# Hybrid encoder layer with a top-2 mixture of experts: the first expert's weight units in buffers of their own, the loop's next units loaded early, and its down product from raw units

## The reference, cut to what matters

```python
h = rmsnorm(x, norm_ffn[i])
# hier_moe: the best of 4 groups, then the best 2 of its 4 experts; 16 experts in all
for e in range(N_EXPERTS):
    gu = t @ w_gate_up[e]                                   # 1024 -> 2 * 256
    y = (jax.nn.silu(gu[:, :D_EXPERT]) * gu[:, D_EXPERT:]) @ w_down[e]   # 256 -> 1024
    out = out + combine[:, e:e + 1] * y
x = x + hier_moe(...)
x = x + jax.nn.sigmoid(x @ w_ple_gate[i]) * rmsnorm(p[i] @ w_ple_proj[i], ple_norm[i])
```

## Time and profile before

| | us |
|---|---|
| median of 3 runs | 652.64 (651.5 to 652.98) |
| the profiled execution, its own time | 650.8 |
| its span, first to last instruction | 649.0 |
| PE busy | 617.4 (95%) |
| DVE busy | 413.1 (64%) |
| ACT busy | 337.6 (52%) |
| POOL busy | 63.1 (10%) |
| mean granted clock of PE | 0.986 of full |

### The profile page before, as it was taken

How to read it: one execution, slowest core, us unless ns; L and a number is a source line. 1 busy time by engine, 2 the same in 40 slices (tenths; PEclk the granted TensorE clock), 3 DMA queues, 4 the chain that set the end, 5 groups by cost and what they waited for, 6 DMA issues and landing times.

```text
span 649.0 us, 8478 instructions
## 1 busy us (share of the span) xinstructions
PE 617.4 (95%) x3088; PEld 501.4 (77%) x3088; DVE 413.1 (64%) x758; ACT 337.6 (52%) x609; POOL 63.1 (10%) x76
## 2 busy tenths in 40 slices
PE   5999999999999999999999986799999999879997
PEld 4878888888887777888788865687777787668885
DVE  6322265444533665656786977788988987866672
ACT  7751222321323665655555664588888886941111
POOL 0000000000000000110011132212122121110000
PEclk9999999999999999999999997799999999989999
DMA  9913205030312430100112659899999999533511
GB/s 346 369 51 149 97 2 191 32 98 1 97 33 65 171 131 0 66 33 34 66 66 81 224 177 342 292 403 400 394 402 397 401 365 339 159 146 114 167 44 66
DMA packets 34506, 113.74 MB, mean 175 GB/s; under 512 B 5240, under 2 KB 5880, under 8 KB 34464
## 3 DMA queue, kind: packets, MB, share of 16 engines
q1 hardware_dynamic: 28752, 99.99, 42.1%
q0 software_dynamic: 4752, 12.59, 5.1%
q10 hardware_dynamic: 960, 0.60, 0.4%
HBM read 103.17 MB, written 14.71 MB: 182 GB/s over the span
## 4 chain that ended last, share of the span: by engine, by line
PE 73%; DVE 13%; ACT 6%; DMA 4%; issue 3%; SPq 0%; ACTq 0%; DVEq 0%; POOLq 0%
PE bank L468 21%; PE bank L470 19%; PE bank L469 19%; DVE w_split L447 7%; PE bank L1721 5%; ACT w_split L441 3%; PE bank L1748 3%; PE bank L1767 3%; DVE moe_xT L1571 2%; PE bank L1729 2%; PE bank L1876 1%; DMA w_raw<-in_w_moe 1%; DMA pick<-moe_rows 1%; ACT s L840 1%; DMA moe_x<-h_rows,slot_token 1%
## 5 line engine op out<-in xcount | busy, mean ns | idle before, releaser
L468 PE MATMUL bank<-w_split,h_T_prompt 128*128 128x512 f32 x192 | 77.6, 404 | 6.7 <-DVE w_split L1186 6.7
L470 PE MATMUL bank<-w_split,h_T_prompt 128*128 128x512 f32 x192 | 75.9, 395 | 0.0
L469 PE MATMUL bank<-w_split,h_T_prompt 128*128 128x512 f32 x192 | 75.8, 395 | 0.0
L463 DVE TENSOR_TENSOR w_split<-w_raw,w_split 128x1024 fp32r<-128x1024 f32 x33 | 40.2, 1221 | 42.2 <-ACT w_split L458 42.1
L447 DVE TENSOR_TENSOR w_split<-w_raw,w_split 128x1024 fp32r<-128x1024 f32 x48 | 56.6, 1220 | 4.8 <-ACT w_split L441 4.7
L468 PE MATMUL bank<-w_split,moe_xT 128*128 128x512 f32 x120 | 50.9, 424 | 6.0 <-DVE moe_xT L1571 3.8
L447 DVE TENSOR_TENSOR w_split<-w_raw_more,w_split 128x1024 fp32r<-128x1024 f32 x44 | 51.8, 1219 | 3.6 <-ACT w_split L441 3.6
L441 ACT ACTIVATE w_split<-w_raw 128x1024 fp32r<-128x1024 f32 x48 | 48.8, 1061 | 0.4
L468 PEld LDWEIGHTS bank<-w_split,h_T_prompt 128*128 128x128 f32 x192 | 36.6, 191 | 15.0 <-DVE w_split L1186 6.7
L470 PE MATMUL bank<-w_split,moe_xT 128*128 128x512 f32 x120 | 48.1, 401 | 0.0
L469 PE MATMUL bank<-w_split,moe_xT 128*128 128x512 f32 x120 | 47.9, 400 | 0.0
(11 more groups left out here) (270 smaller groups left out, 1362.1 us busy)
## 6 DMA issues: line engine op xcount, KB each, us to landing
w_raw<-in_w_moe SPq DMA_DIRECT2D x54, 512.0 KB, 7.4
w_raw_more<-in_w_moe SPq DMA_DIRECT2D x42, 512.0 KB, 8.6
w_raw<-in_w_in SPq DMA_DIRECT2D x24, 512.0 KB, 6.1
pick<-moe_rows SPq DMA_DIRECT2D x10, 512.0 KB, 4.5
w_raw<-in_w_out SPq DMA_DIRECT2D x8, 512.0 KB, 3.4
toep<-bias_table SPq DMA_DIRECT2D x4, 896.0 KB, 7.5
x_row<-in_x SPq DMA_DIRECT2D x6, 512.0 KB, 10.0
x_again<-in_x SPq DMA_DIRECT2D x6, 512.0 KB, 3.2
```

Of the source, the lines that this page charges most:

```text
L463: nc.vector.tensor_tensor(W[:, u % WS, 1], raw(u)[0], f(W[:, u % WS, 0]), ALU.subtract).then_inc(lo_done, 1)
L468: nc.tensor.matmul(out, hi, whi, start=first, stop=False)
L469: nc.tensor.matmul(out, lo, whi, start=False, stop=False)
L470: return nc.tensor.matmul(out, hi, wlo, start=False, stop=last)
```

## The change

The units of expert 15 get raw buffers of their own (`first_raw`, units 0 to 3, in region A), loaded during the attention stage; units 4 and 5 stay in `RAW` and are not split at all. With `RAW` units 0 to 3 free, SP loads the next set as soon as the trip count is known. The down product of a loop trip is made in float32 from the raw units and an unsplit `act32`, so ACT and DVE don't split units 4 and 5 of a trip, nor the transposed product; these raw buffers are refilled once the down half that reads them is done. After the last trip, two more entries of the table name expert 2, so the loop loads units 0 to 3 of t = 3. GpSimd starts the gather of the next loop tile ahead of the loop and at the end of each trip. The order of ACT, DVE and SP follows.

```diff
-C_N = C_SEQ + OVER_TILES + 1
+SETS = OVER_TILES + 2
+C_N = C_SEQ + SETS
-            sb("x2_T_last", [P, KD, P], F32, "A", 8192)]
+            sb("x2_T_last", [P, KD, P], F32, "RAW", 20480)]
-        h2_last = sb("h2_last", [P, D], F32, "A")
+        h2_last = sb("h2_last", [P, D], F32, "RAW", 4096)
+        first_raw = [sb(f"w_raw_first{j}", [P, 2, N], F32, "A", o_)
+                     for j, o_ in enumerate((0, 4096, 40960, 8192))]
+        act32 = sb("loop_actT", [P, 2, P], F32, "X")
-        FIRST_HI = (4, 5, 1, 0, 2, 3)
+        FIRST_HI = (0, 1, 3, 2)
 # SP, ahead of the loop
+            def first_unit(j):
+                sp.dma_start(first_raw[j][:], w_moe[E - 1, j]).then_inc(raw(MOE0 + j)[1], 16)
             for i in range(1, TILES):
+                if i == TILES - 1:
+                    sp.wait_ge(d_s, 2 * (NI - 1))
+                    for j in (0, 1, 3):
+                        first_unit(j)
                 x_again(i)
...
+                sp.wait_ge(lo_done, MOE0 + j - RS + 1)
+                sp.dma_start(RAW[:, (MOE0 + j) % RS], w_moe[E - 1, j]).then_inc(lp_ld[j], 16)
             store_h2(TILES - 2)
+            sp.wait_ge(pe_wo, 2 * TILES - 1)
+            first_unit(2)
             store_h2(TILES - 1)
+            sp.wait_ge(pe_wo, 2 * TILES)
+            moe_unit((2, 1))
+            sp.wait_ge(d_h2, 2 * TILES)
+            moe_unit((2, 3))
             sp.wait_ge(lp_xg, 16)
-            for j in range(2):
+            sp.wait_ge(d_route, 1)
+            n = sp.value_load(trips[0:1, 0:1], min_val=1, max_val=OVER_TILES + 1)
+            src = expert(0)
+            for j in range(4):
+                set_unit(src, j)
+            for j in (2, 0):
+                sp.wait_ge(lp_lo, {0: 4, 2: 3}[j])
                 moe_unit((2, j))
             with sp.Fori(0, n) as i:
-                for j in range(6):
-                    sp.wait_ge(lp_lo, i * 6 + (j + 1))
-                    sp.dma_start(RAW[:, (MOE0 + j) % RS], src[j]).then_inc(lp_ld[j], 16)
-            for j in range(2, 4):
-                moe_unit((2, j))
-            for j in range(4):
-                sp.wait_ge(lp_lo, n * 6 + (j + 1))
+                src = expert(i)
+                for j in range(4, 6):
+                    sp.wait_ge(lp_y, i * 2 + (j - 3))
+                    set_unit(src, j)
+                src = expert(i + 1)
+                for j in range(4):
+                    sp.wait_ge(lp_lo, i * 4 + (j + 5))
+                    set_unit(src, j)
+            for j in range(4, 6):
+                sp.wait_ge(lp_lo, n * 4 + (j + 1))
                 moe_unit((3, j))
             sp.wait_ge(pe_gu, 1)
             for j in range(4, 6):
                 moe_unit((2, j))
 # POOL, ahead of the loop (in the trip the same gather stands after the put)
+            pool.sem_inc(lp_free, 1)
+            pool.tensor_copy(now_u[:], src_u[:, bass.ds(column(0), 1)]).then_inc(g_now, 1)
+            pool.wait_ge(g_now, 2)
+            pool.wait_ge(lp_xt, 2)
+            pool.sem_inc(g_go, 1)
+            fetch(xg[0], now_u[:], lp_xg)
             for i in range(2):
                 pool.wait_ge(gch, 3 + i)
                 gather_x(2 + i)
 # ACT
             ple_out(5)
+            act.wait_ge(lp_lo, 1)
             xT_hi(1)
...
-                out_actT_hi().then_inc(lp_aat, 1)
+                act.activation(act32[:], bank[3][:, 0:DE].rearrange("p (k t) -> p k t", k=2),
+                               ACT.Copy).then_inc(lp_aat, 1)
...
-                for j in range(4, 6):
-                    loop_hi(i, j)
+            for j in range(4, 6):
+                loop_hi(n, j)
             moe_hi((2, 0))
             moe_hi((2, 1))
 # DVE: the table (12 entries before, 13 after)
-            link(dve.tensor_scalar(r_n[:], r_inc[:, E - 1:E], 1.0, None, ALU.add))
+            link(dve.tensor_scalar(r_ep[:], cst[:, C_T:C_T + no], r_inc[:, E - 1:E], 0.0,
+                                   ALU.subtract, ALU.max))
+            link(dve.scalar_tensor_tensor(out=etab[:], in0=r_ep[:], scalar=2.0, in1=r_ea[:],
+                                          op0=ALU.mult, op1=ALU.add))
 # DVE: the loop
             first_lo(0)
+            first_lo(1)
             dve.wait_ge(pe_tab, 2)
...
-            first_lo(1)
+            first_lo(2)
+            first_lo(3)
+            xT_lo(1)
             with dve.Fori(0, n) as i:
-                for j in range(2, 6):
-                    loop_lo(i * 6 + min(j + 3, 6), j)
-                loop_lo(i * 6 + 7, 0)
-                loop_lo(i * 6 + 8, 1)
+                loop_lo(i * 4 + 5, 0)
                 dve.wait_ge(lp_si, i + 1)
                 out_act(0).then_inc(lp_act, 1)
-                dve.wait_ge(lp_aat, i + 1)
-                out_actT_lo().then_inc(lp_dat, 1)
+                loop_lo(i * 4 + 6, 1)
                 for half in range(2):
                     dve.wait_ge(lp_axt, i * 2 + (half + 3))
                     out_xT_lo(half).then_inc(lp_dxt, 1)
+                for j in range(2, 4):
+                    loop_lo(i * 4 + (j + 5), j)
+            for j in range(4, 6):
+                loop_lo(n * 4 + (j + 1), j)
 # PE, the loop's down product
-                pe.wait_ge(lp_dat, i + 1)
+                pe.wait_ge(lp_aat, i + 1)
                 for half in range(2):
-                    pe.wait_ge(lp_lo, i * 6 + (5 + half))
-                    down_half(half, WSLOT[1, 4 + half]).then_inc(lp_y, 1)
+                    pe.wait_ge(lp_ld[4 + half], i * 16 + 16)
+                    w = RAW[:, (MOE0 + 4 + half) % RS]
+                    for k in range(2):
+                        ins = pe.matmul(bank[4 + half][:], act32[:, k], w[:, k], start=(k == 0), stop=(k == 1))
+                    ins.then_inc(lp_y, 1)
```

More of the change, by code:

```diff
@@ L230, in build @@
         r_b, r_inc = rt("r_b", E), rt("r_inc", E)
-        r_et, r_eb = rt("r_et", OVER_TILES + 1, E), rt("r_eb", OVER_TILES + 1, E)
-        r_ef, r_ob, r_cb = (rt(n, OVER_TILES + 1) for n in ("r_ef", "r_ob", "r_cb"))
-        r_n = rt("r_n", 1)
+        r_et, r_eb = rt("r_et", SETS, E), rt("r_eb", SETS, E)
+        r_ef, r_ob, r_cb, r_ea, r_ep = (rt(n, SETS) for n in ("r_ef", "r_ob", "r_cb", "r_ea", "r_ep"))
         p_t = rt("pair_t", 6, E)
@@ L353, in build @@
             "loop_act_silu", "loop_dve_act"))
-        lp_at, lp_aat, lp_dat, lp_y, lp_ay, lp_st = (sem(n) for n in (
-            "loop_pe_actT", "loop_act_actT_hi", "loop_dve_actT_lo", "loop_pe_down", "loop_act_y",
+        lp_at, lp_aat, lp_y, lp_ay, lp_st = (sem(n) for n in (
+            "loop_pe_actT", "loop_act_actT", "loop_pe_down", "loop_act_y",
             "loop_y_stored"))
@@ L434, in moe_raw, with moe_hi @@
             return src, loaded, first + n
-        def moe_hi(unit):
+        def moe_hi(unit, sets=None):
             src, loaded, n = moe_raw(unit)
-            nc.scalar.wait_ge(loaded, 16 * n)
+            if sets is None:
+                nc.scalar.wait_ge(loaded, 16 * n)
+            else:
+                nc.scalar.wait_ge(lp_ld[unit[1]], sets * 16 + 16)
             w_free(nc.scalar, unit)
@@ L980, in first_hi @@
                 slot_free(act, MOE0 + WSLOT[1, j] - 2)
-                src, loaded, k = raw(MOE0 + j)
+                _, loaded, k = raw(MOE0 + j)
                 act.wait_ge(loaded, 16 * k)
-                act.activation(W[:, WSLOT[1, j], 0], src, ACT.Copy).then_inc(lp_hi, 1)
+                act.activation(W[:, WSLOT[1, j], 0], first_raw[j][:], ACT.Copy).then_inc(lp_hi, 1)
             def last_stats(half):
@@ L1001, in _ @@
             act.activation(pTs[0][:], p_raw[:], ACT.Copy).then_inc(a_p, 1)
-            first_hi(4)
+            first_hi(0)
+            first_hi(1)
             last_stats(0)
@@ L1006, in _ @@
             last_stats(1)
-            first_hi(5)
-            first_hi(1)
+            first_hi(3)
             act.wait_ge(g_x2, TILES)
@@ L1105, in _ @@
                 if t < LAST:
-                    moe_hi((t + 1, 2))
-                    moe_hi((t + 1, 3))
+                    moe_hi((t + 1, 2), n if t == 2 else None)
+                    moe_hi((t + 1, 3), n if t == 2 else None)
                 if t > 1:
@@ L1115, in _ @@
                 if t + 2 <= LAST:
-                    moe_hi((t + 2, 0))
-                    moe_hi((t + 2, 1))
+                    moe_hi((t + 2, 0), n if t == 1 else None)
+                    moe_hi((t + 2, 1), n if t == 1 else None)
                 if t > 1:
@@ L1530, in first_lo @@
                 dve.wait_ge(lp_hi, FIRST_HI.index(j) + 1)
-                dve.tensor_tensor(W[:, WSLOT[1, j], 1], raw(MOE0 + j)[0], f(W[:, WSLOT[1, j], 0]),
+                dve.tensor_tensor(W[:, WSLOT[1, j], 1], first_raw[j][:], f(W[:, WSLOT[1, j], 0]),
                                   ALU.subtract).then_inc(lp_lo, 1)
-            no, nl = OVER_TILES + 1, LEVELS + 1
+            no, nl = SETS, LEVELS + 1
             dve.wait_ge(pe_rk, 2)
@@ L1625, in _ @@
                     out_xT_lo(half).then_inc(lp_dxt, 1)
-            xT_lo(1)
```

(6 more changed lines are left out.)

69 lines of the change are left out of this document (30 added, 39 removed).

## The result

The changed kernel takes 647.63 us (median of 15 runs, 644.75 to 648.37), the kernel before 650.62 us in the same comparison (15 runs, 647.6 to 653.16). The ratio is 0.9948, with an interval from 0.993 to 0.9966: faster by 3.0 us by the medians (3.4 by the ratio), where 3.0 were forecast. The level is 2.0 us under the forecast 649.6, because the three runs of before that were shown have a median of 652.64, 2.0 above that of the fifteen (those three included).

The account below looks back on a forecast made before the run. Engines, through a chain of waits with a 9.72 us period, were taken to bound the kernel. t = 2 starting at 413.4 instead of 416.35 gives 3.0 us: 652.64 - 3.0 = 649.6 us, range 647.4 to 653.9.

Parts of the forecast that it names:

- The level: Last step of the sum: median 652.64 of the runs shown, less 3.0, gives 649.6 us; the profiled execution gave 647.8.
- Gate and up: Loop tile: PE's 0.93 us idle before unit 1 goes, 1.15 us with restart; `keep_clock` starts at 392.85.
- Product: Loop tile: next set's loads leave at about 383, silu ends about 393.3, product at 393.75 instead of 399.65.
- Gather: Next loop tile's gather leaves at 390.85, takes 5.0 us, lands at 395.85; PE idles 1.65 us.
- the calm row: Earlier gather landing of 4.1 us in a calmer place, against 6.9 us among six unit loads; 5.0 taken, nearer calm.
- Down product: Loop trip: eight float32 records at 0.43 us, 3.45 us instead of 4.3; t = 1 starts at 400.2, 5.9 us earlier.
- 12 matmuls at half clock: Reading of the down product before the change: 406.08 - 401.76 = 4.3 us, all at half clock.
- Units 4 and 5: Expert 0: loads wait for down halves; unit 5 lands at 404.8, t = 2 starts at 413.4, 3.0 us earlier.
- the gain shrinks: At expert 0's units 4 and 5, late loads cut the 5.9 us head start of t = 1 to 3.0 at t = 2.
- t = 2 to t = 3: Distance kept at 12.3 us, 2.6 over the period, although PE's idle before t = 2 grows from 3.8 to 6.8.
- The period: Static tiles: engines, not transfers, set the 9.72 us step, so an earlier t = 2 moves everything behind it.
- a rival: No change: 400 GB/s paces the static tiles, or longer idle prolongs half clock; 652.0 to 652.9 us, chance 0.15.

Follow-up runs that it names:

- two experiments that removed it: Changed kernel with units 4 and 5 of t = 1 split behind t = 2's units: 645.58 us; with them loaded ahead of the loop into own places: 644.08 us.
- the lighter loads: Half of units 4 and 5 left unloaded in late static tiles: kernel before 649.95 us; three variants of the changed kernel 641.27, 642.71 and 640.2 us.
- two variants with a larger head start: Changed kernel with units 4 and 5 split behind t = 2's units: 645.58 us; the same plus own places loaded ahead of the loop: 643.43 us.
- the fastest variant: Changed kernel with units 4 and 5 loaded ahead of the loop into own places, plus 14 unread matmuls before t = 2: 642.05 us, ratio 0.9878.
- the variant with both orders: Changed kernel with units 4 and 5 loaded ahead of the loop into own places and split behind t = 2's units: 643.43 us, ratio 0.9894.

## Why the prediction came out as it did

The change of 3.0 us and its way were right, and that the figure is exact is luck: steps with errors of opposite sign are behind it, and the lead fell by 4.0 us in one profile of the changed kernel and by 3.2 us in the other. On the scale of the changed kernel (gate and up 1.02 us earlier than before):

- **Gate and up.** The four loads left at 382.72, forecast about 383, which is 382.0 on this scale: 0.7 us late, and nothing waited for them. No idle before unit 1, `keep_clock` at 391.78, forecast 391.83 on this scale. Right.
- **Product.** ACT's three high parts wait for PE's slots alone; silu at 391.98, transposes of the product at 392.88 (forecast 392.7). Right.
- **Gather.** Two errors of opposite sign. It was issued at 390.65, forecast 389.8 on this scale: POOL's copy of the token column started 1.1 us after the slot table was complete, where I had 0.15. It landed in 3.6 us and not 5.0, so the idle was 0.98 instead of 1.65 us. In the nine other profiles whose chain of waits shows it first on its queue it took 3.7 to 4.6 us, around the 4.1 of the earlier trace rows: the calm row was the right one. The rule of the Trainium skill in "DMA: Bandwidth & Descriptors", section "Issuing engines are not separate DMA queues", is neither confirmed nor refuted by these: two loads ran beside the gather in every one of them, and the 5.7 us of the same gather sent third came behind two others of its own engine.
- **Down product.** Eight records in 3.04 us to the next start, 0.38 each, not 0.43; at full clock. The earlier trace rows was the right kind of row, 13% high. The 4.3 us of before were not "12 matmuls at half clock", as I had written: by the earlier trace rows the clock was back at 404.9, and seven were. No term of the sum used it. With the gather this puts t = 1 at 398.26 where the forecast, on this scale, had 399.2.
- **Units 4 and 5.** ACT's wait for unit 5 ended at 403.68, forecast 403.8 on this scale: the 0.9 us won above were lost again, as SP sent the load only 0.5 us earlier than forecast and it took 4.67 us, not 4.3. From there to t = 2 it was 8.44 us, forecast 8.6: t = 2 at 412.12, forecast 412.4. This coupling, named as the place where "the gain shrinks", decided the size, and two experiments that removed it gained 2.0 and 3.5 us more (1.7 and 3.1 by the ratios).
- **t = 2 to t = 3.** Kept at 12.3; 11.55 and 12.15 measured. The longer idle cost nothing more. The rule cited from the Trainium skill, "TensorE: Matmul & The Clock Gate", section "What's actually happening", agrees with the trace: the idle went from 3.77 to 6.95 us and the distance did not grow.
- **The period.** Engines, not transfers, shown by the lighter loads. But the 3.0 us had less room than I saw: at 400 GB/s two variants with a larger head start waited for loads. The earlier trace rows had said so with its share of 1.02, and I used it only as evidence for a rival.

What failed is the level, the last step of the sum: "the predicted time is 652.64 - 3.0 = 649.6 us". The term 652.64 is the median of three runs, and twelve more put it at 650.62, 2.0 us lower. Against that level the forecast 649.6 says 1.0 us faster, and 3.0 were measured. The three had a spread of 1.5 us, and the fifteen one of 5.6, so a median of three could be a microsecond or two off. The profiled execution's own 650.8 was closer, and 650.8 - 3.0 = 647.8 is within 0.2 of the measured time; the text held that number and then replaced it. That a single execution fell so near the median of fifteen is luck too.

## What to carry to other kernels

Where an operand is read straight from its landing buffer to save a copy, the buffer comes free only behind the product, and the next load into it moves back (here by some 3 us); place that load's chain in the sum first. When an edit wins a head start in front of a steady stretch, look how far the second resource stands behind the first (here 400 GB/s at a share of 1.02): in this kernel the engine-paced stretch passed on 7.9 us whole, and of 10.3 us only about half. Between a median of three runs and a profiled execution that disagree, neither is the level; give the range the spread of both.

## What the runs showed of the hardware

- The same indirect gather of 512 KB landed in 3.6 to 4.6 us when it was first on its queue (ten profiles), and in 5.7 us as the third (one profile). What made the difference, the queue or the two gathers ahead, the runs don't separate.
- A full float32 matmul of 128 rows by 512 columns took two records of 0.38 us, 0.76 us, against three fp32r matmuls of 0.23 us, 0.69 us, which it replaces: it saves high and low parts, not time of PE.
- The half clock doesn't follow the idle alone, and it can begin after the restart. In the fastest variant PE idled 2.08 us ahead of the loop's transposes and stayed at full clock; in the variant with both orders it idled 1.72 us, and the clock fell 1.1 us after it had restarted, so that the down product took 5.29 instead of 3.60 us:

```profile
394.85 1.09 PE L1773 MATMUL bank<-cst,moe_x 128*128 128x128 f32 x8 [1.72 <-DMA moe_x<-h_rows,tile_tokens]
395.78 5.29 PE L2133 MATMUL bank<-w_raw,loop_actT 128*128 128x512 f32 x8
```

```profile
395.50:396.00 0.50, 0.50 (x6) 0.48 (x4) 0.00 (x0) 0.46 (x1) 0.00 (x0) 0.92 0.78 197
396.00:396.50 0.50, 0.50 (x2) 0.01 (x1) 0.33 (x1) 0.50 (x2) 0.00 (x0) 0.50 0.77 221
```

- The stretch at half clock behind a restart is not fixed either: in t = 2 it took 3.9 us in one execution of the changed kernel and 5.3 us in another, with idles of 6.95 and 6.77 us.
